# Last sparse tile: V rows gathered pick by pick and summed with per-token weights on VectorE, phases of 18, 18, 17 and 11 iterations

## The reference

```
h = einsum('td,ted->te', x, u[expert])          # 128 dot products of 1024 for each token
a = gelu(h) * gate
y = einsum('te,ted->td', a, v[expert])          # weighted sum of 128 rows of v for each token
x2 = LayerNorm(ALPHA * x + y)
```

## Time and profile before

| | us |
|---|---|
| median of 3 runs | 3359.24 (3352.19 to 3367.15) |
| the profiled execution: its own time | 3360.03 |
| its span (first to last instruction) | 3358.4 |
| `experts`, phase 0 (iterations 0 to 17) | 1590 to 2077 |
| phase 1 (18 to 35) | 2077 to 2555 |
| phase 2 (36 to 53) | 2555 to 3033 |
| phase 3 (54 to 63) | 3033 to 3321 |
| end: last sums, layer norm, output | 3321 to 3358 |

### The profile page before, as it was taken

How to read it: one execution, slowest core, us unless ns; L and a number is a source line. 1 busy time by engine, 2 the same in 40 slices (tenths; PEclk the granted TensorE clock), 3 DMA queues, 4 the chain that set the end, 5 groups by cost and what they waited for, 6 DMA issues and landing times.

```text
span 3358.4 us, 39617 instructions
## 1 busy us (share of the span) xinstructions
PE 2814.9 (84%) x14408; PEld 2187.2 (65%) x14408; DVE 2310.0 (69%) x4936; ACT 932.6 (28%) x1295; POOL 1587.4 (47%) x1196
## 2 busy tenths in 40 slices
PE   7996799996988546564466999999999999999996
PEld 6896788885766446553244667676667776766664
DVE  4511666651899989996576777777877777775445
ACT  4311322321444434342111222222222222222221
POOL 0000000101577755553666664666665667653543
PEclk9987899997988777877788999999999999999998
DMA  3323211202211059998999998999999999997984
GB/s 129 106 71 97 71 44 56 66 13 102 71 48 35 32 180 305 302 303 232 404 393 387 388 390 328 397 394 386 377 385 342 401 381 391 391 355 280 343 331 175
DMA packets 383433, 829.65 MB, mean 247 GB/s; under 512 B 158080, under 2 KB 180992, under 8 KB 383264
## 3 DMA queue, kind: packets, MB, share of 16 engines
q0 software_dynamic: 150864, 548.60, 42.7%
q1 hardware_dynamic: 232400, 278.84, 24.8%
HBM read 768.49 MB, written 58.85 MB: 246 GB/s over the span
## 4 chain that ended last, share of the span: by engine, by line
PE 15%; DMA 13%; POOL 12%; DVE 8%; issue 4%; ACT 0%; POOLq 0%; DVEq 0%; ACTq 0%
DMA e_u_row<-in_u,id_u 11%; POOL hold L1775 8%; POOL e_u_row L1766 4%; DVE e_u_row L1979 3%; PE psum L1837 3%; PE psum L1802 2%; PE psum L1823 2%; PE psum L1803 2%; PE psum L1804 2%; PE psum L1824 2%; PE psum L1825 2%; DMA hold<-in_v,id_v 2%; DVE e_y L1970 1%; DVE e_ul L1937 1%; DVE e_vl L1941 1%
## 5 line engine op out<-in xcount | busy, mean ns | idle before, releaser
L1775 POOL DMA_INDIRECT hold<-in_v,id_v x512 | 577.3, 1128 | 316.2 <-PE psum L1837 172.8
L1979 DVE CUSTOM_DVE_ANT_0 e_u_row<-e_u_row,hold 128x1024 f32<-128x1024 f32 x384 | 467.9, 1223 | 280.7 <-DMA e_u_row<-in_u,id_u 249.9
L1766 POOL DMA_INDIRECT e_u_row<-in_u,id_u x384 | 482.9, 1257 | 372.5 <-DVE hidden_s L1979 241.3
L1823 PE MATMUL psum<-e_vh,e_ah 128*128 128x512 f32 x1024 | 425.1, 415 | 114.2 <-DVE e_y L1970 83.1
L1824 PE MATMUL psum<-e_vl,e_ah 128*128 128x512 f32 x1024 | 412.3, 403 | 0.0
L1825 PE MATMUL psum<-e_vh,e_al 128*128 128x512 f32 x1024 | 410.1, 400 | 0.0
L1970 DVE TENSOR_TENSOR e_y<-e_y,psum 128x512 f32<-128x512 f32 x504 | 327.7, 681 | 82.7 <-PE psum L1825 57.3
L1823 PEld LDWEIGHTS psum<-e_vh,e_ah 128*128 128x128 f32 x1024 | 199.9, 195 | 230.3 <-DVE e_y L1970 103.3
L1802 PE MATMUL psum<-x1d_hi,e_uh 128*128 128x512 f32 x864 | 342.7, 397 | 0.0
L1803 PE MATMUL psum<-x1d_lo,e_uh 128*128 128x512 f32 x864 | 337.5, 391 | 0.0
L1804 PE MATMUL psum<-x1d_hi,e_ul 128*128 128x512 f32 x864 | 336.4, 389 | 0.0
(11 more groups left out here) (319 smaller groups left out, 5534.0 us busy)
## 6 DMA issues: line engine op xcount, KB each, us to landing
e_vr<-in_v SPq DMA_DIRECT2D x128, 512.0 KB
e_ur<-in_uT SPq DMA_DIRECT2D x108, 512.0 KB
s_G<-g_tile SPq DMA_DIRECT2D x8, 4096.0 KB, 29.6
e_g<-s_G SPq DMA_DIRECT2D x128, 256.0 KB
p_wr<-in_w_ch SPq DMA_DIRECT2D x17, 512.0 KB, 3.8
s_ch<-p_out POOLq DMA_DIRECT2D x16, 512.0 KB, 3.8
m_ch<-s_ch SPq DMA_DIRECT2D x8, 1024.0 KB, 5.9
r_w<-in_wq SPq DMA_DIRECT2D x16, 512.0 KB
```

Of the source, the lines that this page charges most:

```text
L1766: pool.indirect_dma_start(out=u_ring[n % U_RING][:], out_offset=None, in_=io["u"], in_offset=bass.IndirectOffsetOnAxis(ap=id_u[:, s, k:k + ...
L1775: pool.indirect_dma_start(out=v_ring[m % V_RING], out_offset=None, in_=io["v"], in_offset=bass.IndirectOffsetOnAxis(ap=id_v[:, t:t + 1], a ...
L1823: nc.tensor.matmul(acc, ah[s][j][:, r], vh[s][j][:, c], start=(j == 0), stop=False)
L1979: nc.vector.tensor_tensor_reduce(row, row, xs[:, s, :], 1.0, 0.0, ALU.mult, ALU.add, hs[:, s, k:k + 1]).then_inc(dotted, 1)
```

## The change

Phase 3 begins one iteration earlier (53 in place of 54), so that phase 2 has 17 iterations and phase 3 has 11. The V rows of sparse tile 3 are no longer gathered token by token and summed on PE. POOL gathers them pick by pick (partition = token, by `id_u`), and DVE multiplies each block with the token's weight (a per-partition scalar, `hs[:, 3, n:n+1]`) and adds it to one of two running sums: `totals[0]` is the tile's x times ALPHA in place, `totals[1]` is the first U buffer, zeroed. A sum waits for the one two before it (the last one on the same total). The ring is three U buffers and eight V buffers, 11 in all. The 128 sums lie in DVE's eight slots per iteration, from iteration 53.25 to 64. PE's transpose, ACT's weight columns and the 32 `weigh_rows` of tile 3 go.

```diff
-PHASE = (0, 18, 36, 54, 64)
+PHASE = (0, 18, 36, 53, 64)
...
-        for s in range(NS):
+        for s in range(NS - 1):
             for at, ns in spread(PHASE[s] + 0.5, PHASE[s + 1] - 0.1, 32, V_SLOTS).items():
                 steps[at] = [32 * s + n for n in ns]
+        STEPS = 32 * (NS - 1)
+        sums = spread(PHASE[NS - 1] + 0.25, PHASE[NS], P, U_SLOTS)
+        sum_ring = u_ring[1:] + v_ring
+        S_RING = len(sum_ring)
+        totals = (xs[:, NS - 1, :], u_ring[0][:])
...
+                def gather_last(n):
+                    if n >= S_RING:
+                        pool.wait_ge(summed, n - S_RING + 1)
+                    elif n < U_RING - 1:
+                        pool.wait_ge(dotted, P * (NS - 1) - U_RING + n + 2)
+                    else:
+                        pool.wait_ge(weighted, STEPS - 1 + (n - U_RING + 1) // 4)
+                    pool.indirect_dma_start(out=sum_ring[n % S_RING][:], out_offset=None, in_=io["v"],
+                                            in_offset=bass.IndirectOffsetOnAxis(ap=id_u[:, NS - 1, n:n + 1], axis=0)
+                                            ).then_inc(s_landed[n % S_RING], 16)
...
+                for n in range(P):
+                    gather_last(n)
...
-                        if c == 0 and g in PHASE[:NS]:
+                        if c == 0 and g in PHASE[:NS - 1]:
                             turn(PHASE.index(g))
...
                 def dot_rows(g, c):
 
+                    sum_rows(g, c)
...
+                def sum_rows(g, c):
+
+                    for n in sums.get((g, c), []):
+                        dve.wait_ge(s_landed[n % S_RING], 16 * (n // S_RING + 1))
+                        if n >= 2:
+                            dve.wait_ge(summed, n - 1)
+                        nc.vector.scalar_tensor_tensor(totals[n % 2], sum_ring[n % S_RING][:], hs[:, NS - 1, n:n + 1],
+                                                       totals[n % 2], ALU.mult, ALU.add).then_inc(summed, 1)
...
+                        if s == NS - 1:
+                            nc.vector.tensor_scalar(totals[0], totals[0], ALPHA, None, ALU.mult)
+                            nc.vector.memset(totals[1], 0.0).then_inc(scaled, 1)
+                            dve.wait_ge(s_gated, NS)
+                            dve.wait_ge(scaled, 1)
...
-                add_rows(NS - 1)
+                dve.wait_ge(summed, P)
+                for n in range(2):
+                    c = slice(n * HALF, (n + 1) * HALF)
+                    nc.vector.tensor_tensor(totals[0][:, c], totals[0][:, c], totals[1][:, c], ALU.add).then_inc(s_added, 1)
```

More of the change, by code:

```diff
@@ L1693, in experts @@
         v_landed = [sem(f"v_rows_landed{n}") for n in range(V_RING)]
+        s_landed = [sem(f"last_row_landed{n}") for n in range(U_RING - 1 + V_RING)]
         dotted = sem("u_row_dotted")
         weighted = sem("v_rows_weighted")
+        scaled, summed = sem("last_rows_scaled"), sem("last_row_summed")
         cleared, centred = sem("column_cleared"), sem("column_centred")
@@ L1915, in _ @@
                             split_u(g + 1, j)
-                        if j == 0 and starts is not None:
+                        if j == 0 and starts is not None and starts < NS - 1:
                             act.wait_ge(s_turned, starts + 1)
```

## The result

The changed kernel takes 3331.92 us (median of 7 runs, 3330.08 to 3344.32) against 3362.64 us for the kernel before on the same chip: a ratio of 0.9912, 95% interval 0.9897 to 0.9927. It is 0.9% faster.

What follows compares the result with a forecast made beforehand. The prediction took phase 2 as bound by the gathers, with PE close behind, and phase 3 by PE, then DVE after the change. 3360.0 - 7.6 (phase 2) + 2 (phase 3) gave 3354 us, no change, range 3337 to 3373.

Steps and rivals of the forecast that it cites:

- Phase 2, one iteration less: Phase 2: gathers decide at 392 GB/s, so it takes 470 us, 7.6 less than 477.6.
- phase 2 goes with PE: Rival, chance 0.25: DMA has slack the schedule left unused, 405 GB/s holds, phase 2 takes 456 us, total 3340.
- Phase 3 on DVE: Phase 3: DVE's dense work, 128 sums at 1.20 us and the start make 290 us, 2 us longer than now.
- the round trip to ACT: Phase 3 on DVE: 0.3 us added per iteration, between L1953 and L1957, which a single-sum slot only just covers.
- PE and the clock: Rival, chance 0.06: pauses in phase 3 lower PE's clock to 0.80, 27.3 us an iteration, total 3364.
- DVE's sums cost more: Rival, chance 0.12: semaphore waits put phase 3's sums 1.43 us apart, phase 3 grows by 29 us, total 3384.
- the rival by the rule of the Trainium skill: Rival, chance 0.02: every DVE instruction costs its whole length without overlap, phase 3 takes 315 us, total 3379.
- POOL and the ring: Phase 3's gathers: 117 at 2.27 us are 266 us, less than 290, so POOL costs nothing even at its worst.
- The end: End of the kernel: two additions replace two L1987, `values(63)` waits for the last `e_vl` as now; no change.
- The sum: Whole kernel: 3360.0 less 7.6 in phase 2 plus 2 in phase 3, forecast 3354 us, no change.

Runs made afterwards that it cites:

- run 3: The kernel before with only POOL's gather order changed, always four U blocks and then one group of four V blocks: 3321.9 us, ratio 0.9883.
- run 9: The changed kernel with only phase 2's gather order made worse, runs of six U blocks and then two: 3367.2 us, ratio 1.0021 against the kernel before.
- run 10: The changed kernel with all sums on one total, each waiting for the one just before: 3344.2 us, ratio 0.9956.
- run 8: The changed kernel with DVE's sums covering only columns 0 to 511, every gather kept: 3293.2 us, ratio 0.9802.

## Why the prediction was wrong, point by point

- *Phase 2, one iteration less.* This step failed. I took 392 GB/s as what the DMA engines give over a longer time, since two stretches agreed on it (and 10.42 MB in 26.57 us). Both follow lists made by the same sort, with runs of six, and neither was flat: in run 3 173 us of the early stretch move 405. The even phase holds slices of 405 to 410, and another order alone moves phase 2 from 454.5 to 484.7 us (run 9). The 456 that I had worked out for the rival "phase 2 goes with PE" was close to the right number, for another reason: the gathers still decide, at 405. So the rival had half of it: the slack was there, but PE does not set the phase in the changed kernel (busy for 443 of 454 us), and what had left the slack unused was the order of the list: with all else as before, run 3 takes 12.6 us less in this phase, and there PE is full. My reading of the earlier trace rows was the error; in the dip of 328 and 301 POOL issued nothing for 6 us, and the share of 0.98 over the phase hid a stretch of 0.49. The row was there: the earlier trace rows show DVE before U rows, and POOL's own waits for DVE in the same stretch I did not follow up. What I counted was the blocks per iteration, not how they stand in POOL's list.
- *Phase 3 on DVE.* Right: 1.20 us a sum, 11.8 us of dense work, 26.1 an iteration. The phase took 285.6 where I had 290; the 3.3 us for the round trip to ACT were not needed, and the wait for the gelu at the start was 3.2 as before (3011.96 - 3008.73).
- *PE and the clock.* PE is busy for 251 of 285 us at a granted clock of 0.96. Pauses of up to 3.3 us occur, and behind the one that ends at 3129.66 the granted clock is at its lower level (1.2 GHz) for 3.4 us: matmuls start 0.43 us apart in place of 0.23. DVE hides it. The rival fell.
- *DVE's sums cost more.* The rival fell: with a wait for the sum two back they start 1.20 us apart, as forecast. Run 10 shows the price where each waits for the last one, 0.18 us for a pair. Starts 1.13 us apart for 1.22 us instructions stand in phase 3 too, so the rival by the rule of the Trainium skill (page "VectorE: DVE Perf Modes", section "The DRAIN you can't avoid") fell as well; what that section adds, that an operation which is not held starts earlier, agrees with the 1.13.
- *POOL and the ring.* Right in effect: gathers of 1.51 us, 117 x 1.81 = 212 us of 285, and no sum that waited for a landing.
- *The end.* I said nothing would change; it was 2.0 us shorter. Open.
- *The sum.* Of the 23 us between 3354 and the 3331 of the profiled execution, phase 2 has 15.5, phase 3 4.4, the end 2.0, and 1.4 lie ahead of phase 2.

## What to carry to other kernels

Where one engine issues transfers for several consumers in one list, look at the longest stretches in which it issues nothing, and at what stands behind the transfer it waits for. Runs longer than the ring went with starved DMA engines here. Neither the sum of the waits shows it (58.1 us before, 55.7 in run 3; the longest are 6.1 and 2.5) nor a DMA share of 0.98. Spread work so that the count per iteration is whole, or cap the runs in the list; capping alone was worth 40 us here, more than the change. A mean rate is a capacity only if its slices are flat; where they alternate between a plateau and dips, the plateau is the better estimate, and the dips have a cause to look for.

## What the runs showed of the hardware

- One core's DMA engines held 405 to 410 GB/s in slices of 11 us one behind the other in phase 2 after, with gathered rows of 4 KB as three quarters of the bytes, and 405 GB/s over 173 us in run 3.
- A scalar_tensor_tensor of 128x1024 with a per-partition scalar costs 1.20 us in a row of others (after), 1.38 when it waits for the one just before it (run 10).
- Gathers on POOL took 1.03 us on average beside a DVE that is busy for 128 of 288 us, and 1.51 beside one busy for 283 of 285; in run 8, with half of each sum, 1.20 beside 198 of 216 (127.60 us for 106). What makes them longer no run isolates.
